# Feed-forward down product as seven block products instead of eight, with the block sums on GpSimd and x turned in two halves

## What is computed

```python
def swiglu_ffn(h, w_gate, w_up, w_down):
    return (jax.nn.silu(h @ w_gate) * (h @ w_up)) @ w_down

for l in range(DEPTH):                      # DEPTH = 2
    x = x + 0.5 * swiglu_ffn(rms_norm(x, ffn1_norm[l]), ffn1_w_gate[l], ffn1_w_up[l], ffn1_w_down[l])
    ...                                     # mixer
    x = x + 0.5 * swiglu_ffn(rms_norm(x, ffn2_norm[l]), ffn2_w_gate[l], ffn2_w_up[l], ffn2_w_down[l])
```

## Time and profile before

| | |
|---|---|
| median of three runs | 1618.95 us (1618.14 to 1619.02) |
| profiled execution | 1619.11 us, span 1617.2 us |
| TensorE matmul busy | 1482.7 us, 92% |
| VectorE busy | 1004.6 us, 62% |
| ScalarE busy | 702.9 us, 43% |
| GpSimd busy | 67.6 us, 4% |
| mean granted TensorE clock | 0.967 |

### The profile page before, as it was taken

How to read it: one execution, slowest core, us unless ns; L and a number is a source line. 1 busy time by engine, 2 the same in 40 slices (tenths; PEclk the granted TensorE clock), 3 DMA queues, 4 the chain that set the end, 5 groups by cost and what they waited for, 6 DMA issues and landing times.

```text
span 1617.2 us, 28426 instructions
## 1 busy us (share of the span) xinstructions
PE 1482.7 (92%) x10839; PEld 1159.5 (72%) x10840; DVE 1004.6 (62%) x1858; ACT 702.9 (43%) x1216; POOL 67.6 (4%) x88
## 2 busy tenths in 40 slices
PE   9999999999999999999999999999999776666666
PEld 7888888888888888888888889888854333333333
DVE  6777788677777777788677767988743321222122
ACT  6555566555555555666555556856320000000000
POOL 0000040000001000030200000001000000000000
PEclk9999999999999999999999999999999988888788
DMA  9665365365555655363465654454999999999997
GB/s 325 205 206 182 114 236 193 105 218 187 191 185 171 220 181 192 103 234 130 152 208 183 206 182 157 131 182 145 402 395 414 428 431 432 433 425 434 429 433 311
DMA packets 150205, 407.91 MB, mean 252 GB/s; under 512 B 5360, under 2 KB 98912, under 8 KB 140032
## 3 DMA queue, kind: packets, MB, share of 16 engines
q1 hardware_dynamic: 148800, 404.28, 67.6%
q0 software_dynamic: 1344, 2.80, 0.8%
HBM read 406.00 MB, written 1.05 MB: 252 GB/s over the span
## 4 chain that ended last, share of the span: by engine, by line
PE 73%; DMA 19%; DVE 4%; ACT 2%; issue 1%; SPq 0%; DVEq 0%; ACTq 0%
PE bank L2125 20%; DMA expert_gu<-in_exp_gu 18%; PE bank L2131 10%; PE bank L2084 10%; PE bank L2085 10%; PE bank L2086 10%; PE bank L2746 5%; DVE wlo L1285 1%; PE bank L2766 1%; PE bank L2675 1%; DMA raw<-in_ffn_w_up 1%; PE bank L2701 1%; PE bank L2457 0%; ACT whi L830 0%; DVE small L1430 0%
## 5 line engine op out<-in xcount | busy, mean ns | idle before, releaser
L1285 DVE TENSOR_TENSOR wlo<-raw,whi 128x1024 fp32r<-128x1024 f32 (+1 forms) x396 | 449.0, 1182 | 65.2 <-ACT whi L830 65.0
L830 ACT ACTIVATE whi<-raw 128x1024 fp32r<-128x1024 f32 (+1 forms) x396 | 382.7, 1021 | 69.5 <-PE bank L2086 68.1
L2125 PE MATMUL bank<-hboth,whi 128*128 128x512 f32 x1408 | 350.6, 391 | 1.9 <-DVE hboth L1328 1.4
L2125 PEld LDWEIGHTS bank<-hboth,whi 128*128 128x128 f32 x1408 | 258.3, 188 | 53.5 <-issue 2.0
L2746 PE MATMUL bank<-expert_gu,h_e 128*32 128x256 f32 x1984 | 155.4, 481 | 115.1 <-DMA expert_gu<-in_exp_gu 110.3
L2746 PEld LDWEIGHTS bank<-expert_gu,h_e 128*32 128x32 f32 x1984 | 76.7, 137 | 193.1 <-issue 173.5
L2131 PEld LDWEIGHTS bank<-hboth,wlo 128*128 128x128 f32 x1408 | 191.6, 190 | 13.4
L2131 PE MATMUL bank<-hboth,wlo 128*128 128x256 f32 x1408 | 195.7, 282 | 0.0
L2021 DVE SCALAR_TENSOR_TENSOR e_sg<-e_th,bank 128x128 f32<-128x128 f32 x33 | 9.5, 287 | 288.7 <-ACT e_th L1241 288.7
L2084 PE MATMUL bank<-whi,hboth 128*128 128x512 f32 (+2 forms) x384 | 150.3, 391 | 1.4 <-DVE hboth L1328 0.9
L2086 PE MATMUL bank<-whi,hboth 128*128 128x512 f32 (+2 forms) x384 | 146.8, 382 | 0.0
(11 more groups left out here) (392 smaller groups left out, 1779.5 us busy)
## 6 DMA issues: line engine op xcount, KB each, us to landing
expert_gu<-in_exp_gu SPq DMA_DIRECT2D x24, 4096.0 KB, 38.1
expert_dn<-in_exp_dn SPq DMA_DIRECT2D x29, 2048.0 KB, 38.7
raw<-in_ffn_w_gate SPq DMA_DIRECT2D x44, 1024.0 KB, 5.5
raw<-in_ffn_w_up SPq DMA_DIRECT2D x44, 1024.0 KB, 7.4
raw<-in_ffn_w_down SPq DMA_DIRECT2D x44, 1024.0 KB, 4.9
raw<-in_w_in SPq DMA_DIRECT2D x36, 1024.0 KB, 5.2
expert_gu<-in_exp_gu SPq DMA_DIRECT2D x8, 2048.0 KB, 18.6
expert_gu<-in_exp_gu SPq DMA_DIRECT2D x10, 1024.0 KB, 8.5
```

What stands on the lines that cost most here:

```text
L830: nc.scalar.activation(slot_view(whi, slot, src), src, ACT.Copy).then_inc(hi_ready, inc)
L1285: nc.vector.tensor_tensor(slot_view(wlo, slot, src), src, slot_view(whi, slot, src).bitcast(F32), ALU.subtract).then_inc(lo_ready, inc)
L2125: nc.tensor.matmul(out_[:], wh[:, k, :], hboth[:, k, :, :], start=k == 0, stop=False, skip_group_check=True)
```

## The change

The chunks are taken in 11 pairs. With e and o the even and the odd chunk of a pair, t the row tile (0, 1) and h the half of the output columns, the pair's part of the down product is a 2 x 2 by 2 x 2 block product: (A_te) by (B_eh), (B_oh). It is written in Winograd's form with seven block products P1 to P7 in place of eight. Each of the seven is summed over all pairs in a bank of its own, and x is made from the seven at the stage's end.

- Weights: four differences of 512 columns for a pair, on GpSimd, two of them written over the landed block in `raw`, two into `tt`. Three slots for a pair (six blocks) are split where there were two; the seventh block (`e`) of all pairs is loaded again as a batch of its own (`k == PAIRS`) and split into five and a half slots more at the end. The positions of a stage become 83 where they were 66.
- Activations: GpSimd now scales up (`up_r`) and forms the product of sg and up (256 columns each, for each chunk), and four sums of 128 columns for a pair. ScalarE and VectorE split them in three steps for a pair: 256, 256 and 384 columns.
- TensorE: two block products for a pair at a time (`down_first`, `down_second`), seven for the last pair, and the 11 products of P3 (`third`) at the end. Gate and up have one bank each, so gate of a chunk waits until VectorE has read gate of the chunk before.
- End of a stage: ScalarE, VectorE and GpSimd form x from the seven banks (four additions of 512 columns on GpSimd), the left half of x is turned before the last products of P3, and the right half between the first products of the next stage.
- GpSimd's table loads move into the feed-forward before the mixer, at the second pair; the load of `kept_dn` (2 MB) moves from the first mixer to the third.
- SyncE's, ScalarE's, VectorE's and TensorE's loops over chunks are written out.

```diff
+            def ffn(i):                                   # GpSimd
...
+                def weight_sums(p):
+                    b11, b12, _, b22 = blocks_of(p)
+                    t1, t2 = tt[:, p % 2, 0, :], tt[:, p % 2, 1, :]
+                    gp.wait_ge(raw_landed[(b + p) % 2][2], batch_value(b + p))
+                    if p >= 2:
+                        gp.wait_ge(lo_ready, ffn_pos(i, "s", p - 2, 2) + 1)
+                    V.tensor_tensor(t1, b12, b11, ALU.subtract).then_inc(wsum_made, 1)
+                    gp.wait_ge(wsum_made, 4 * (R + p) + 1)
+                    V.tensor_tensor(t2, b22, t1, ALU.subtract).then_inc(wsum_made, 1)
+                    V.tensor_tensor(b12, b22, b12, ALU.subtract).then_inc(wsum_made, 1)
+                def last_weight_sum(p):
+                    _, _, b21, b22 = blocks_of(p)
+                    gp.wait_ge(wsum_made, 4 * (R + p) + 3)
+                    V.tensor_tensor(b22, tt[:, p % 2, 1, :], b21, ALU.subtract).then_inc(wsum_made, 1)
+                def hidden(c):
+                    p, o = c // 2, c % 2
+                    A = acts[:, p % 2, :, :]
+                    gp.wait_ge(window_step, window_done(z, c, "up"))
+                    V.tensor_tensor(up_r[:, o, :], up_b[:, o, :], rcol[:], ALU.mult).then_inc(hidden_step, 1)
...
+                    V.tensor_tensor(dst, sg[:, o, :].rearrange("p (t c) -> p t c", t=T), up_r[:, o, :].rearrange("p (t c) -> p t c", t=T),
+                                    ALU.mult).then_inc(hidden_step, 1)
...
+                    if o == 0:
+                        V.tensor_tensor(A[:, 1, :], A[:, 0, :], A[:, 4, :], ALU.subtract).then_inc(hidden_step, 1)
+                        return
+                    V.tensor_tensor(A[:, 5, :], A[:, 4, :], A[:, 3, :], ALU.add).then_inc(hidden_step, 1)
...
+                    V.tensor_tensor(A[:, 6, :], A[:, 5, :], A[:, 0, :], ALU.subtract).then_inc(hidden_step, 1)
...
+                    V.tensor_tensor(A[:, 7, :], A[:, 2, :], A[:, 6, :], ALU.subtract).then_inc(hidden_step, 1)
...
+                hidden(0)
+                for q_ in range(1, PAIRS):
+                    hidden(2 * q_ - 1)
+                    weight_sums(q_)
+                    hidden(2 * q_)
+                    last_weight_sum(q_)
+                    if q_ == 2 and nxt and nxt[0] == "mid":
+                        load_mid(nxt[1])
...
+                hidden(2 * PAIRS - 1)
+                for (t, h), add, ready in (((0, 0), u_p, (u_ready, z + 1)), ((1, 0), v_p, (wv_ready, 2 * z + 2)),
+                                           ((1, 1), v_p, (wv_ready, 2 * z + 2)), ((0, 1), w_p, (wv_ready, 2 * z + 1))):
+                    gp.wait_ge(*ready)
+                    half = x[:, t, h * 512:(h + 1) * 512]
+                    V.tensor_tensor(half, half, add[:], ALU.add).then_inc(added_ready, 1)
...
+                for q_ in range(1, PAIRS):                # VectorE
+                    last = q_ == PAIRS - 1
+                    split("g", 2 * q_ + 1)
+                    split("u", 2 * q_ + 1)
+                    low_odd(q_ - 1)
+                    gate(2 * q_)
+                    split("s", q_ - 1, 2)
+                    sigmoid(2 * q_)
+                    low_sums(q_ - 1)
+                    up(2 * q_)
+                    if not last:
+                        split("g", 2 * q_ + 2)
+                        split("u", 2 * q_ + 2)
+                    else:
+                        split("e", 0)
+                    low_even(q_)
+                    if not last:
+                        split("s", q_, 0)
...
+                    gate(2 * q_ + 1)
+                    split("s", q_, 0 if last else 1)
+                    sigmoid(2 * q_ + 1)
+                    up(2 * q_ + 1)
+                split("s", p, 1)
+                split("s", p, 2)
+                low_odd(p)
+                low_sums(p)
+                split("e", 3)
+                split("e", 4)
...
+                first_gate_up()                           # TensorE
+                gate_up(1)
+                for q_ in range(1, PAIRS):
+                    gate_up(2 * q_)
+                    down_first(q_ - 1)
+                    gate_up(2 * q_ + 1)
+                    down_second(q_ - 1)
+                for n in range(3):
+                    third(n)
+                down_last(PAIRS - 1)
+                third(3)
+                turn(i + 1, 0)
+                third(4)
+                third(5)
```

More of the change, by code:

```diff
@@ L588, in _ @@
                 if st[0] == "ffn":
[L589 to L596, removed]
+                    for k in range(batches(i)):
+                        ffn_batch(i, k, before[k] if k < 2 else last_use(i, k - 2))
+                        if i == 0 and k == 2:
+                            load_constants()
                 else:
@@ L2174, in ffn @@
-                f4 = first4(m)
-                first_gate_up(f4[0], f4[1])
-                gate_up(1, f4[2], f4[3], f4[2], f4[3], scale=True)
-                def chunk(c, o, first=False):
-                    down(c, o, m + 3 * c, m + 3 * o, first, False)
-                    gate_up(o, m + 3 * c + 1, m + 3 * c + 2, m + 3 * o + 1, m + 3 * o + 2)
-                chunk(0, 0, True)
-                chunk(1, 1)
-                with pe.Fori(0, 9) as r:
-                    for o in range(2, 4):
-                        chunk(r * 2 + o, o)
@@ L2187, in ffn, with first_gate_up @@
-                down(20, 20, m + 60, m + 60, False, False)
-                down(21, 21, m + 63, m + 63, False, True)
+                def first_gate_up():
+                    mg, mu = ffn_pos(i, "g", 0), ffn_pos(i, "u", 0)
+                    gate, up = ((bank[3], *parts(mg), mg, 1), (bank[5], *parts(mu), mu, 2))
+                    for some in (range(0, 4), range(4, KC)) if after_ffn(i) else (range(KC),):
+                        if some[0]:
+                            turn(i, 1)
+                        for both in ([(gate,), (up,)] if i == 0 else [(gate, up)]):
+                            for _, _, _, mm, _ in both:
+                                pe.wait_ge(hi_ready, mm + 1)
+                            for k in some:
+                                pe.wait_ge(hlo_ready, turned(i) + k + 1)
+                                for out_, wh, _, _, _ in both:
+                                    high_product(out_, wh, k)
+                        for out_, _, wl, mm, used in (gate, up):
+                            low_products(out_, wl, mm, used, some)
@@ new lines, in third @@
+                def third(n):
+                    pos = ffn_pos(i, "e", n)
+                    pe.wait_ge(lo_ready, pos + 1)
+                    if n == 0:
+                        pe.wait_ge(window_step, window_done(z, 2 * PAIRS - 1, "gate"))
+                    for p in range(2 * n, min(2 * n + 2, PAIRS)):
+                        ins = product(P3, *sums(p, 2), pos, p % 2, p == 0, p == PAIRS - 1)
+                    ins.then_inc(split_used if n < 5 else y_ready, 1)
+                first_gate_up()
```

640 lines of the change are left out of this document (428 added, 212 removed).

## The result

The changed kernel takes 1847.15 us (median of four runs, 1846.27 to 1849.3) against 1618.89 before: ratio 1.1413, 95% interval 1.1393 to 1.1433. It is 228 us slower; 1796 was forecast, with 1635 to 1860 as the range, so the measured time lies inside it, 13 us from its upper end.

What follows compares the result with a forecast made beforehand. TensorE bounded the kernel before; after the change VectorE and GpSimd, excluding each other, would. A stage: head 12.7, ten pairs of 20.0, end 16, 228.7 against 185.7, +43.0; four times +172, table loads +5: 1796 us, range 1635 to 1860.

Steps and rivals of the forecast that it cites:

- Exclusion and its floor: Feed-forward pair: GpSimd's SBUF operations and VectorE's two-SBUF-input operations never run side by side; holds of 8.2 and 9.4 sum to 17.6 us.
- The two narrow rows: GpSimd multiplications of 32 and 64 columns in the old trace, ending 0.12 and 0.18 us behind VectorE splits, read as exclusion.
- GpSimd's rate: GpSimd in a pair: 2.1 ns a column, so 1.14, 0.60 and 0.33 us for 512, 256 and 128 columns.
- The rival of quick wide operations: Wide GpSimd operations at 1.55 ns a column or less, so TensorE bounds: -7 us a stage, 1592 us; chance 0.15.
- The pair: Two chunks of a feed-forward: VectorE's 12.8 plus GpSimd's 8.2, less overlaps, plus 0.8 of waits: 20.0 us, range 17.6 to 21.5.
- TensorE's saving and VectorE's 12.8: Running pair: TensorE falls from 16.6 to 15.2 us; VectorE's own work rises from 11.9 to 12.8 us.
- 11.7 + 1.0: Head of a feed-forward: 11.7 us as before, plus 1.0 for turning the right half of x between products.
- the end's 16: End of a feed-forward: next stage's first product about 16 us behind the last up product, where before it was 7.9.
- What the halves save: Turning x in two halves at a stage's end: saves at most 0.45 us of waiting.
- the case that had set that edge: Likeliest case, chance 0.75, upper end: pair of 21.5 us, head 12.7, end 17; 245 us a stage, 1855 us in all.
- The clock: Rival: waiting TensorE granted a lower clock, 0.85, pair work 17.9 us under 20.0; adds 1 to 3 us a stage, at ends only.
- The moved loads: Table loads in GpSimd's queue, three stages, 3.8 us each, about half felt: +5 us; load of kept_dn 0, uncovered at most 4.9.

Runs made afterwards that it cites:

- the runs with reads and with writes on the kernel before: Kernel before plus GpSimd operations nothing waits for, twelve a pair: reading additions 1732.6 us, ratio 1.0709; memsets of about equal GpSimd time instead, 1617.62 us, ratio 0.9999.
- with nothing wide on GpSimd: Changed kernel with all twelve GpSimd operations of a pair over one column, 1635.99 us; for the 39 us, also additions into x and fill later, 1631.07 us.
- with all on VectorE: Changed kernel with all twelve GpSimd operations of a pair moved to VectorE, same result, additions into x left on GpSimd: 1763.44 us, ratio 1.0897.
- narrow differences: Changed kernel with the four weight differences of a pair made over 1 column in place of 512, a fill added at each stage's head: 1717.47 us, ratio 1.0612.
- the run with everything narrow: Changed kernel with all twelve GpSimd operations of a pair and the additions into x over one column, fill behind the row scale: 1631.07 us, ratio 1.0075.
- the run with both halves late: Changed kernel with both halves of x turned behind the feed-forward's last product, before the next stage's first product: 1861.37 us, ratio 1.1495 to the kernel before.

## Why the prediction was right, and what it mis-sized

**Exclusion and its floor.** Right. The two narrow rows carried the argument, and the runs with reads and with writes on the kernel before show it in isolation: +114 us against none. In the changed kernel the differences of 512 columns have medians of 2.28 us (L843) and 1.36 (L845) and maxima over 2, as forecast. The rule of the Trainium skill ("SBUF — State Buffer", Who interferes with whom), reads against two-input operations and not writes, agrees with both.

**GpSimd's rate.** Right. 512, 256 and 128 columns with nothing in the way take 1.26, 0.73 and 0.46 us (minima of L845 and L859, and L869), 2.1 ns a column, where the earlier trace rows ended at 64 columns. The rival of quick wide operations is dead by that.

**The pair.** 20.0 forecast, 19.85 measured, by parts that were off against each other, so that the close number is in part luck. The standing, from the means over their unhindered lengths: splits 280 x 0.28, sg 88 x 0.49, sums 44 x 0.98, even parts 44 x 0.55, splits of `tt` 44 x 0.21: 198 us, 4.5 a pair, where I had 6.4 (8.2 less 1.8). The waits of VectorE for the chain (74.3 for the even part, 48.3 for the odd) are 2.8 a pair, where I had 0.8. GpSimd, standing itself, lengthens the chain (up_r 1.64 us for 0.73), and VectorE idles while that lasts; what it idles, it does not stand.

**TensorE's saving and VectorE's 12.8.** Right: the pair is 15.30 us with nothing wide on GpSimd, VectorE is busy in 12.73 of it, and it is 17.96 with all on VectorE for 18.2 summed.

**The ends.** This is where the difference from 1796 to 1847 lies. In the four stages the heads are 77.4 us for 50.8 forecast and the ends 94.6 for 64, 57 us over; the pairs are 782.8 for 800, 17 under. The rest of the span is 15.5 us over the kernel before, where the sum had only 5 us for the table loads. The mis-sized terms are the head, "11.7 + 1.0", the end's 16, and the turn of the right half in the stage that follows, for which the 1.0 stood: each mixer waits 3.3 to 3.5 us for a split behind it (shown above). What the halves save was mis-sized too: 3.6 us a stage net, not 0.45 at most.

At the head GpSimd makes the first pair's differences directly behind the root of the norm, beside VectorE's scaling and copies of the roots (VectorE, then GpSimd, third feed-forward):

```profile
610.69 1.23 DVE L1560 TENSOR_SCALAR nr<-nr 128x2 f32<-128x2 f32 x1 [0.60 <-POOL nr L791]
...
611.89 1.42 DVE L1564 COPY rb<-nr 128x128 f32<-128x128 f32 x2
...
610.63 1.25 POOL L843 TENSOR_TENSOR tt<-raw 128x512 f32<-128x512 f32 x1
611.96 1.26 POOL L845 TENSOR_TENSOR tt<-raw,tt 128x512 f32<-128x512 f32 x1
```

Scaling and copies take 1.23 and 1.42 us where they take 0.17 and 0.36 with narrow differences. TensorE waited 1.32 us for the right half of `hboth` and 3.63 for the copy of the roots (1.48 in the run with everything narrow), then ran gate at the lower of its two clock levels (eight products in 3.76 us for 2.0; granted clock 0.55 from 614.24 to 619.10). Behind the head, in the first pair, it waited 2.25 us for gate's bank.

At the end TensorE waited 3.05 us before the third factor's first product for the window of the last gate, 1.8 for the sums' low part, 1.3 for x, 1.0 for the last split. I had counted the end from the last window, but TensorE had run ahead of it: VectorE read the last gate 4 us behind the last up product.

**The range.** The measured time lies at its upper edge, and not by the case that had set that edge: 1855 stood for a pair of 21.5 with an end of 17, and what came was a pair under 20 with heads of 18.6 to 20.5 and ends of 22.7 to 24.9. That the overrun of the ends stayed inside a range made for the pair is luck.

**The clock.** 0.93 in the ten pairs. It does not set the pair: TensorE still idles in 30 of the 198 us. Nor does a wait alone bring it, since the kernel before with GpSimd's reads has 1.00 in the pairs of its third feed-forward, with 18.8 us for a pair where TensorE's work is 16.6. Its share at the heads and ends was not separated.

**The moved loads.** They were not tried alone, but the traces show little. The table loads (5 us forecast) stand in GpSimd's queue at 662.10 to 665.88, where GpSimd otherwise waits for up (4.10 us in the pair before, 0.39 in this one), and the pair there is 19.80 us like its neighbours; the one pair of the fourth feed-forward in whose queue eight small multiplications stand (5.85 us) is 20.65. For `kept_dn` (0 forecast): from the end of the fourth feed-forward to the end of the span the run with both halves late takes 645.3 us and the kernel before 642.9, so 2.4 us is all that it and the rest of the change can cost there.

## What to carry to other kernels

Before work is given to GpSimd, sum what GpSimd reads and what VectorE does with two SBUF inputs as if they were one engine; if the sum is over the bound, the idle engine is no help, and VectorE alone may be faster (here 18.0 us a pair against 19.8). Memsets of GpSimd beside VectorE's two-input operations, and GpSimd's reads beside operations of VectorE with an input in PSUM, cost nothing here. And a saving in the running part must be carried through the head, the end and the start of the next stage: with nothing wide on GpSimd the pairs of four stages gave 39 us and these three took 51. The sums were tried on GpSimd and on VectorE only.

## What the runs showed that I had not expected

- VectorE's scaling and copy of the roots, which have one input tensor, are held by GpSimd's fills, which only write: the scaling at 506.20 takes 3.49 us in place of 0.17, with two memsets of 1.8 us beside it that began 0.07 before it, and the copies behind it 3.48 in place of 0.36, while two-input operations of VectorE don't feel memsets at all (1222 ns). Whether the copies were held themselves or only stood behind the scaling this row doesn't show. The Trainium skill's page "SBUF — State Buffer", Who interferes with whom, has VectorE's copy and scaling by a scalar among those that can take the shared pair of ports; the row agrees.
- In the run with reads on the kernel before, the narrowest GpSimd operations suffer most: 128 columns take a mean of 1309 ns for 0.46 alone, 256 columns 843 for 0.73. In the stretch read there the six end at 114.20, well into VectorE's three splits, which start at 111.25, so the last ones, the narrow ones, meet whole splits.
